# Three small lone stages of a two-block transformer kernel are taken into their neighbours

## The reference, cut to what matters

```
h = x
proj = rmsnorm(h, norm_mix_g) @ w_in            # q, k, v, u
h = h + concat(rmsnorm(attention), rmsnorm(ssm)) @ w_out
h = h + memory_attention(rmsnorm(h), rmsnorm(mem))
h = h + peer(rmsnorm(h))
...
mod = silu(c) @ w_ada + b_ada                   # shifts sh, scales sc, gates g
h1 = rms_norm(h, norm1_g) * (1 + sc1) + sh1     # norm2 likewise with sc2, sh2
ang = positions * inv_freq;  cos, sin = cos(ang), sin(ang)
q, k = rope(rms_norm(q, qn)), rope(rms_norm(k, kn))
lam = exp(lam_q1 . lam_k1) - exp(lam_q2 . lam_k2) + 0.2
```

## Time and profile before

| | |
|---|---|
| timed executions, median | 3892.75 us |
| the profiled execution: span from its first to its last event | 3886.6 us |
| PE busy | 3642.7 us (94%) |
| DVE busy | 2969.4 us (76%) |
| ACT busy | 1709.3 us (44%) |
| POOL busy | 737.9 us (19%) |
| DMA | 853.09 MB, mean 219 GB/s |

### The profile page before, as it was taken

How to read it: one execution, slowest core, us unless ns; L and a number is a source line. 1 busy time by engine, 2 the same in 40 slices (tenths; PEclk the granted TensorE clock), 3 DMA queues, 4 the chain that set the end, 5 groups by cost and what they waited for, 6 DMA issues and landing times. The chain is left out here.

```text
span 3886.6 us, 54799 instructions
## 1 busy us (share of the span) xinstructions
PE 3642.7 (94%) x19550; PEld 3183.2 (82%) x19550; DVE 2969.4 (76%) x6481; ACT 1709.3 (44%) x3206; POOL 737.9 (19%) x523
## 2 busy tenths in 40 slices
PE   7877899999999999999798999989999999999998
PEld 6545677899999988888687766778999999888887
DVE  3654463599888889999677576444998888799998
ACT  3512343234566643333354455332335666533333
POOL 0000000000333334444100000000002333345442
PEclk9978999999999999999898999999999999999999
DMA  4261222355899999999532102222557999899997
GB/s 130 84 217 44 87 90 76 115 163 167 272 309 307 304 344 405 404 402 399 194 99 64 65 8 76 65 87 96 163 166 238 314 309 310 306 402 404 404 404 285
DMA packets 371790, 853.09 MB, mean 219 GB/s; under 512 B 36016, under 2 KB 185136, under 8 KB 368944
## 3 DMA queue, kind: packets, MB, share of 16 engines
q1 hardware_dynamic: 258816, 530.45, 39.3%
q0 software_dynamic: 73728, 268.47, 18.2%
q10 hardware_dynamic: 38976, 50.68, 3.8%
HBM read 753.91 MB, written 94.37 MB: 218 GB/s over the span
## 5 line engine op out<-in xcount | busy, mean ns | idle before, releaser
L1150 POOL DMA_INDIRECT p2f_row<-in_expert_u_rows,p2f_index x128 | 174.4, 1362 | 1351.1 <-POOLq L83 1078.2
L1150 POOL DMA_INDIRECT p1f_row<-in_peer_u_rows,p1f_index x128 | 179.5, 1402 | 1006.8 <-POOLq L83 707.8
L1766 PE MATMUL p2v_out<-p2a_u_hi,p2v_w_hi 128*128 128x512 f32 x768 | 299.2, 390 | 0.4 <-DVE p2v_w_lo L1747 0.4
L1766 PE MATMUL p1v_out<-p1a_u_hi,p1v_w_hi 128*128 128x512 f32 x768 | 299.2, 390 | 0.0
L1766 PE MATMUL p2v_out<-p2a_u_lo,p2v_w_hi 128*128 128x512 f32 x768 | 299.2, 390 | 0.0
L1766 PE MATMUL p1v_out<-p1a_u_hi,p1v_w_lo 128*128 128x512 f32 x768 | 299.2, 390 | 0.0
L1766 PE MATMUL p1v_out<-p1a_u_lo,p1v_w_hi 128*128 128x512 f32 x768 | 299.2, 390 | 0.0
L1766 PE MATMUL p2v_out<-p2a_u_hi,p2v_w_lo 128*128 128x512 f32 x768 | 299.1, 390 | 0.0
L1150 POOL DMA_INDIRECT p2f_row<-in_expert_v,p2f_index x128 | 203.5, 1590 | 238.1 <-DVE p2f_sum L1173 217.2
L1725 ACT CAST p1a_u_hi<-p1a_u 128x1024 fp32r<-128x1024 f32 x128 | 135.1, 1055 | 254.9 <-PE p1v_out L1766 246.6
L1150 POOL DMA_INDIRECT p1f_row<-in_peer_v,p1f_index x128 | 175.3, 1370 | 235.1 <-DVE p1f_sum L1173 213.8
(11 more groups left out here) (737 smaller groups left out, 10905.9 us busy)
## 6 DMA issues: line engine op xcount, KB each, us to landing
p1a_u<-in_peer_u SPq DMA_DIRECT2D x128, 512.0 KB, 4.3
p1a_u<-in_peer_v SPq DMA_DIRECT2D x128, 512.0 KB, 9.4
p2a_u<-in_expert_u SPq DMA_DIRECT2D x128, 512.0 KB, 4.1
p2a_u<-in_expert_v SPq DMA_DIRECT2D x128, 512.0 KB, 10.1
gates<-p_kept SPq DMA_DIRECT2D x20, 2048.0 KB, 12.0
acts<-p1a_a ACTq DMA_DIRECT2D x128, 192.0 KB, 4.3
p1w_a<-acts SPq DMA_DIRECT2D x128, 192.0 KB, 7.9
acts<-p2a_a ACTq DMA_DIRECT2D x128, 192.0 KB, 4.3
```

The lines of the kernel that those rows point to most:

```text
L1150: self.nc.gpsimd.indirect_dma_start(self.row[:, n % self.RING, :], None, self.u_rows if dot else self.v_rows, bass.IndirectOffsetOnAxis(ap ...
L1766: last = nc.tensor.matmul(out[:, o, :], lhs[:, s, t * P:(t + 1) * P], rhs[:, n % VSLABS, cols], start=(n == 0 and m == 0), stop=(n == KEYS ...
```

## The change

- x is loaded in four parts of 512 KB, one for each token tile, issued by SP in the first stage (now `opening`) right behind `cols`. The stage doesn't wait for them; in n0, ACT waits for part t before it squares tile t. The stage `load` is gone. The four semaphores belong to the outermost level and are cleared at the end of the program.
- The stage `rope_tables` is gone. `RopeTables`, a guest of w1, does its work in slabs 1 to 7 of the first chunk, in space of `mixT`, which is free until the attention. n0's `transfers` load its positions and `rows` (now 544 columns, 272 KB, since the gains aren't repeated). Behind w1's last slab, SP stores the tables (1 MB) to DRAM and waits, ahead of the bias; n3's `transfers` load them back in place of the 1936 KB of rows.
- The stage `scales` is gone: its two scale columns are made in `take_columns`, behind a wait for its own four additions, and `subln` beside `att_q` in the first stage.
- `mem` is loaded by n1's `transfers` instead of at the head of wmq. This isn't in the change's short title, but it is in the diff.

```diff
         self.copied = [sem("nm_copied_by_act"), sem("nm_copied_by_dve")]
         self.out = out
     def load(self, sp):
-        sp.dma_start(self.mem[:], self.mem_dram).then_inc(self.mem_in, 16)
+        pass
...
     def act(self, act, slab):
         if slab in (1, 2):
             t = slab - 1
-            act.wait_ge(self.mem_in, 16)
             if t == 1:
                 act.wait_ge(self.squared, 1)
...
             for t in range(tiles):
+                if arrived:
+                    act.wait_ge(arrived[t], 16)
                 nc.scalar.activation(xn[:, t, :], src[:, t, :], ACT.Square,
                                      accum_out=sumsq[:, t:t + 1]).then_inc(squares_done, 1)
...
-for _name, _width in (("gains", 2 * DIL_W + 2 * DIFF_W), ("inv_freq", HEAD // 2), ("lambdas", 4 * HEAD)):
+for _name, _width in (("gains", 4 * HEAD), ("inv_freq", HEAD // 2), ("lambdas", 4 * HEAD)):
...
-def constants(nc, ctx, cols_dram):
+def opening(nc, ctx, cols_dram, h, x_dram, arrived):
...
         @block.sync
         def _(sp):
             sp.dma_start(cols[:], cols_dram).then_inc(cols_in, 16)
+            for t in range(TT):
+                sp.dma_start(h[:, t, :], x_dram[:, t, :]).then_inc(arrived[t], 16)
...
             nc.vector.tensor_scalar(att_q[:], cols[:, a:a + 1], HEAD ** -0.5, None, ALU.mult)
+            nc.vector.tensor_scalar(subln[:], cols[:, b:b + 1], 1.0 - LAM_INIT, None, ALU.mult)
...
                 hT = phase_tools(nc, ctx, "b1n")[0]("hT", [P, DK, SEQ])
-                norm_transpose(nc, "n0", C, h, TT, D, hT, column(C, "norm_mix_g"))
+                rope = RopeTables(nc, A, mixT, lam_neg)
+                norm_transpose(nc, "n0", C, h, TT, D, hT, column(C, "norm_mix_g"), transfers=rope.sources(),
+                               arrived=arrived)
...
+                        ahead=rope.store, inside=[rope, heads])
...
-        memory_attention(nc, C, h, hT, A)
+        sb, _, _ = phase_tools(nc, ctx, "b1m")
+        hT, mem = sb("hT", [P, DK, SEQ]), sb("mem", [P, MEM_LEN // P, D])
+        norm_transpose(nc, "n1", C, h, TT, D, hT, column(C, "norm_mem_g"),
+                       transfers=[(mem[:], A["mem"].rearrange("(t p) d -> p t d", p=P))])
+        memory_attention(nc, C, h, hT, mem, A)
...
+                                         self.C["cols"][:, ab + 8 * src:ab + 8 * src + 8],
+                                         ALU.add).then_inc(self.columns_taken, 1)
+        dve.wait_ge(self.columns_taken, MODS)
+        for i, name in enumerate(("norm1_g", "norm2_g")):
+            a = COLS[name][0]
+            self.nc.vector.scalar_tensor_tensor(self.C["scales"][:, i, :], self.mods[:, 2 * i + 1, :], 1.0,
+                                                self.C["cols"][:, a:a + 8], ALU.add, ALU.mult)
...
+class RopeTables:
...
+    def store(self, sp):
+        sp.wait_ge(self.made, 1)
+        sp.dma_start(self.A["rope"], self.tables).then_inc(self.stored, 16)
+        sp.wait_ge(self.stored, 16)
...
+    def act(self, act, slab):
+        if slab == 3:
+            act.wait_ge(self.ready, 1)
+            self.nc.scalar.activation(self.sinb, self.red, ACT.Sin).then_inc(self.sined, 1)
+            self.nc.scalar.activation(self.s_half, self.half, ACT.Sin).then_inc(self.sined, 1)
+        if slab == 4:
+            self.nc.scalar.activation(self.edots, self.dots, ACT.Exp).then_inc(self.exped, 1)
...
+    def tables_of(self, kinds):
+        for kind in kinds:
+            gain = self.rows[:, kind * HEAD:(kind + 1) * HEAD].unsqueeze(1).broadcast_to([P, TT, HEAD])
+            for half in range(2):
+                cols = slice(self.F * half, self.F * half + self.F)
+                for table, angle in ((self.cosg, self.cosb), (self.sing, self.sinb)):
+                    last = self.nc.vector.scalar_tensor_tensor(table[:, :, kind, cols], angle, KIND_SCALES[kind],
+                                                               gain[:, :, cols], ALU.mult, ALU.mult)
+        return last
...
+    def dve(self, dve, slab):
+        V, F = self.nc.vector, self.F
+        if slab == 1:
+            self.ch = ch = Chain(dve, self.v)
+            f0, l0 = ROWS["inv_freq"][0], ROWS["lambdas"][0]
+            ch.add(V.tensor_copy(self.posf, self.posi))
+            lams = self.rows[:, l0:l0 + 4 * HEAD].rearrange("p (a b d) -> p a b d", a=2, b=2)
+            ch.add(V.tensor_tensor(self.prod, lams[:, :, 0, :], lams[:, :, 1, :], ALU.mult))
...
+            ch.add(V.tensor_reduce(self.dots, self.prod, AX.X, ALU.add))
+            ch.add(V.tensor_tensor(self.ang, self.posf.unsqueeze(2).broadcast_to([P, TT, F]),
+                                   self.rows[:, f0:f0 + F].unsqueeze(1).broadcast_to([P, TT, F]), ALU.mult))
...
+        if slab == 2:
+            sincos_reduced(V, self.ch, self.ang, self.turns, self.red)
+            V.tensor_scalar(self.half, self.red, 0.5, None, ALU.mult).then_inc(self.ready, 1)
...
+        if slab == 5:
+            ch = self.ch
+            dve.wait_ge(self.sined, 2)
+            ch.add(V.tensor_tensor(self.sq, self.s_half, self.s_half, ALU.mult))
             ch.wait()
+            ch.add(V.tensor_scalar(self.cosb, self.sq, -2.0, 1.0, ALU.mult, ALU.add))
+            dve.wait_ge(self.exped, 1)
+            ch.add(V.tensor_tensor(self.diff, self.edots[:, 1:2], self.edots[:, 0:1], ALU.subtract))
...
+            V.tensor_scalar(self.lam_neg[:], self.diff, -LAM_INIT, None, ALU.add)
+        if slab == 6:
+            self.tables_of((0, 1))
+        if slab == 7:
+            self.tables_of((2, 3)).then_inc(self.made, 1)
...
         qkT = sb("qkT", [P, QK2_TILES, SEQ])
-        lam_neg = sb("lam_neg", [P, 1])
         with ExitStack() as ctx:
-            sbr, _, _ = phase_tools(nc, ctx, "b2r")
-            cosg, sing = (sbr(n, [P, TT, len(GAIN_AT), HEAD]) for n in ("cosg", "sing"))
-            with ExitStack() as ctx2:
-                rows = phase_tools(nc, ctx2, "b2s")[0]("rows", [P, NROWS])
-                norm_transpose(nc, "n3", C, h, TT, D, hT, lambda k: scale1[:, k:k + 1], lambda k: mods[:, 0, k:k + 1],
-                               transfers=[(rows[:], A["rows"].partition_broadcast(P))])
-                rope_tables(nc, C, A, cosg, sing, rows, lam_neg)
+            rope = phase_tools(nc, ctx, "b2r")[0]("rope", [P, 2, TT, len(GAIN_AT), HEAD])
+            cosg, sing = rope[:, 0], rope[:, 1]
+            norm_transpose(nc, "n3", C, h, TT, D, hT, lambda k: scale1[:, k:k + 1], lambda k: mods[:, 0, k:k + 1],
+                           transfers=[(rope[:].rearrange("p a t k d -> p (a t k d)"), A["rope"])])
             queries_keys(nc, C, hT, A["w_qk_2"], cosg, sing, qkT)
         oaT = sb("oaT", [P, 2, SEQ])
...
 def program(nc, A, stop=None):
     with ExitStack() as ctx:
-        C = constants(nc, ctx, A["cols"])
-        sb, _, _ = phase_tools(nc, ctx, "main")
+        sb, _, sem = phase_tools(nc, ctx, "main")
         h = sb("h", [P, TT, D])
-        load(nc, "x", [(h[:], A["x"].rearrange("(t p) d -> p t d", p=P))])
+        arrived = [sem(f"arrived{t}") for t in range(TT)]
+        C = opening(nc, ctx, A["cols"], h, A["x"].rearrange("(t p) d -> p t d", p=P), arrived)
         mods = sb("mods", [P, MODS, DK])
         g1 = sb("g1", [P, D])
         g2 = sb("g2", [P, D])
         C["scales"] = sb("scales", [P, 2, DK])
-        C["subln"] = sb("subln", [P, 1])
-        block1(nc, C, h, A, Modulation(nc, C, A, mods, g1, g2))
-        scales(nc, C, mods)
-        block2(nc, C, h, mods, g1, g2, A)
+        lam_neg = sb("lam_neg", [P, 1])
+        block1(nc, C, h, A, arrived, Modulation(nc, C, A, mods, g1, g2), lam_neg)
+        block2(nc, C, h, mods, g1, g2, A, lam_neg)
```

More of the change, by code:

```diff
@@ L990, in _, with norm_transpose @@
                 finish(dve, i)
-def norm_transpose(nc, tag, C, src, tiles, width, dst, scale, bias=None, transfers=()):
+def norm_transpose(nc, tag, C, src, tiles, width, dst, scale, bias=None, transfers=(), arrived=()):
     kt = width // P
@@ L2335, in column, with block1 @@
     return lambda k: C["cols"][:, a + k % width:a + k % width + 1]
[L2338 to L2353 removed]
+def block1(nc, C, h, A, arrived, modulation, lam_neg):
     with ExitStack() as mid:
@@ new lines, with __init__, sources, place @@
+class RopeTables:
+    F = HEAD // 2
+    def __init__(self, nc, A, space, lam_neg):
+        self.nc, self.A, self.lam_neg = nc, A, lam_neg
+        flat = space[:].rearrange("p a b -> p (a b)")
+        self.tables = flat[:, 0:ROPE]
+        self.cosg, self.sing = (flat[:, n * ROPE // 2:(n + 1) * ROPE // 2].rearrange("p (t k d) -> p t k d", t=TT, d=HEAD)
+                                for n in range(2))
+        self.rows = flat[:, ROPE:ROPE + NROWS]
+        at = ROPE + 2 * BANK
+        self.posi = flat[:, at + 900:at + 900 + TT].bitcast(I32)
+        spare = lambda n: flat[:, at + TT * self.F * n:at + TT * self.F * (n + 1)].rearrange("p (t f) -> p t f", t=TT)
+        (self.ang, self.turns, self.red, self.half, self.s_half, self.sq) = (spare(n) for n in range(6))
```

(30 more changed lines are left out.)

109 lines of the change are left out of this document (20 added, 89 removed).

## The result

In the comparison that gave the result, the changed kernel took 3868.14 us (median of 6 runs, 3860.58 to 3870.84) and the kernel before 3887.47 us (median of 6, 3877.93 to 3895.26): 0.995 of the time, interval 0.9937 to 0.9963, 19.3 us less. The forecast of 3869.7 us was 1.6 us off. Two errors cancel in that: the gain was to be 23 us and was 19, and the starting point, 3892.75 us from three runs, was 5 us above what more runs of the same kernel give (3887.69 us, median of 29). So that the figure came out within 1.6 us is luck; what can be judged is the gain, 19.3 against 23.05 us. One run of the kernel before in the second group of experiments, 4204.72 us, fell into a slower state and is left out.

What follows compares the result with a forecast made beforehand. PE is busy 94% of the span, so only its idle time between stages can be won. Terms -8.0, -5.05, -0.6, -10.5, +0.5 and +0.6 sum to -23.05 us, giving a 3869.7 us median; range 3862 to 3877 us.

Steps and rivals of the forecast that it cites:

- Opening: Program start through n0: x issued earlier in four parts lets everything behind start sooner, -8.0 us (bounds -8.7 and -6.5).
- third square: n0 on ACT: third square ready at 8.95 us, where today the rehearsal starts at 16.98 us.
- rival of parts in a row: Opening: x's four parts don't overlap, last at 11.6 to 17.0 us; time 3871 to 3878 us; chance 0.09.
- Guest in w1: First chunk of w1: the rope-table work fits beside the product, DVE 17.9 and ACT 12.2 of 21.76 us; cost 0.
- tight place of the forecast: Head of w1: slab 3's `w_lo` ready at 38.4 us, PE there at 40.1 us, 1.7 us to spare.
- rival of a late w1: w1's first chunk: DVE becomes the bound; 3895 us at twice the guest's price; chances 0.03 late, 0.02 late and slower.
- wmq: Start of wmq without `mem` ahead: first split 3.1 us sooner and 1.95 us from the clock, -5.05 us.
- the clock's, -1.95 us: First matmuls of wmq: with shorter idle time PE comes back at full instead of half clock, -1.95 us.
- `scales` and `rope_tables`: Around block 2: removing both stages gains their time on the timeline, -0.6 and -10.5 us.
- Program's end: After the last stage: clearing x's four semaphores with one more barrier costs +0.5 us (0 to 0.8).
- Clock at the moved starts: Starts of wmq and qk: one chance in six each of a 1.7 us clock loss, +0.6 us (0 to 3.4).
- sign of being wrong: Second trace: another stage gets longer though nothing in it was edited; no size given.

Runs made afterwards that it cites:

- after_one_x: Changed kernel with x loaded as one 2 MB DMA in the first stage instead of four parts: 3872.0 us, 0.9966 of the kernel before.
- after_long: Changed kernel with 18 instead of 10 pairs of rehearsal matmuls at most product starts: 3869.21 us, 0.9947 of the kernel before.
- before_long: Kernel before with 18 instead of 10 pairs of rehearsal matmuls at most product starts: 3888.73 us, 1.0003 of the kernel before.
- long_double: after_long with the guest's angle reduction and 16 table products in w1 done twice: 3871.76 us (one run).
- opening_only: Kernel before with only the four early loads of x, awaited tile by tile in n0: 3884.96 us, 0.9996 of the kernel before.
- rope_scales_only: Kernel before with only the rope tables and scale columns moved; x's stage and mem's place unchanged: 3883.87 us, 0.999 of the kernel before.
- mem_only: Kernel before with only the load of mem moved from the head of wmq to n1: 3881.96 us, 0.9986 of the kernel before.
- before_again: Kernel before, unedited, run and profiled a second time: 3884.72 us (one run).
- before_bridge: Kernel before with three more rehearsal pairs after the first weight slab lands, at each product's start: 3883.7 us, 0.9992 of the kernel before.
- after_again: Changed kernel, unedited, run and profiled a second time: 3868.59 us, 0.9945 of the kernel before.

## Why the prediction was right

**Opening, forecast -8.0 us: measured -7.9 and -7.3** (w1 at 19.31 and 20.1 against 27.21 and 27.4 us). The third square was to be ready at 8.95 us, the rehearsal started at 8.79; the transposes were to start near 13.3, they did at 13.21. The assumption that carried it, that four parts move as the one does, holds: 7.7 against 7.9 us here, 8.5 at most in the other traces. The rival of parts in a row (the last at 11.6 us or later) is out. The Trainium skill ("DMA: Bandwidth & Descriptors", Bandwidth), which wants 1 MiB and more for each DMA, would have kept the one load; after_one_x is that version, its w1 starts 3 to 4 us later, and its median is 3.4 us higher.

**Guest in w1, forecast 0: measured 0.** In after_long, where the clock is full, w1 takes 99.4 us against 99.3 in before_long, and PE never waits in chunk 0. These are its eight slabs, in the columns of the earlier trace rows, and the tight place of the forecast:

```profile
25.13:46.89 21.76, 21.73 (x96) 18.03 (x97) 16.82 (x48) 11.82 (x21) 0.00 (x0) 1.00 0.53 174
...
27.70 1.28 ACT L2666 ACT_TABLE_LOAD   x1
30.27 0.31 ACT L2666 ACTIVATE b_mixT<-b_mixT 128x128 f32<-128x128 f32 x1 [1.29 <-DVE b_mixT L2697]
...
30.76 0.68 DVE L284 TENSOR_TENSOR w_w_lo<-w_w,w_w_hi 128x512 fp32r<-128x512 f32 x1
```

DVE is busy for 16.8 us (forecast 17.9), ACT for 11.8 (12.2). The sine does wait for DVE, and slab 3's `w_lo` ends at 31.44 us; PE needs it at 25.16 + 3 x 2.72 = 33.3 us, 1.9 us to spare where the forecast had 1.7. In after, the root's table comes back at 89.13 us and still leaves ACT 0.53 us of waiting for PE before its next split, and the bias is issued at 87.78 us, 5.7 us behind the store of the tables: both as estimated, and hidden. The rival of a late w1 put the point at which it decides at 1.5 times the guest's work, and 25 us of loss at twice: at 12 us of guest in place of 7, long_double shows one wait and w1 0.7 us longer, with PEclk 1.00 before and behind it. That rival's price was far too high, since one short wait at the end of the guest's work isn't one in every slab.

**wmq, forecast -5.05 us: measured -3.4.** The term that was mis-sized is the clock's, -1.95 us. (Its own figures, nine intervals and a first one, add up to -2.06; with full clock restored, wmq is 1.3 to 1.8 us shorter still, 51.8 to 52.0 against 53.3 to 53.6 us.) I reasoned that idle time of 2.27 us leaves the clock full because w1 showed it once. One row in one trace can't say that: w1 itself was hit in five of eight unbridged traces.

**`scales` and `rope_tables`, forecast -11.1 us: measured -10.6** (544.9 us on average in the seven traces without the two stages, 555.5 us in the seven with them). qk starts 0.7 us behind n3's last copy. In `take_columns` the two products end at 260.9 us and `take_row` behind them idles 2.06 us for PE: covered.

**Program's end, forecast +0.5 us: measured +0.4 to 0.5** (from the first store of `out` to the end of the span 17.7 to 17.8 us against 17.3).

**Clock at the moved starts, forecast +0.6 us: too small, and wrong in kind.** I looked only at wmq and qk. Nearly half of all such starts are hit, in both kernels, each for 1.6 to 2 us (w1 101.0 against 99.4, pa 18.9 against 17.3, gl 103.7 against 102.1, vb 52.3 against 50.3). In the traces shown, after has six hits and the first of before had one. This is the sign of being wrong that I had named, a stage longer though nothing in it was edited: va and vb are. And the change isn't neutral in it, since it takes the half-clock rehearsal from qk. The four unbridged traces with the stage `rope_tables` have 15 hits together, the four without it 19: one more each, or some 1.7 us (my estimate, from these counts and the price of a hit; four traces on either side can't show so small a difference).

These terms sum to -7.9 - 3.4 - 10.6 + 0.5 = -21.4 us; the two traces of after are 17.5 and 19.8 us shorter than the first of before, and the medians 19. The 2 to 4 us between are within what the clock and the ssm tables (102.1 to 110.4 us, over both kernels alike; `take_columns`, some 0.4 us on DVE, is the only edit there) do to a run.

**What stays open.** The single edits' medians don't add up. opening_only gives 1.3 us, rope_scales_only 3.8, mem_only 4.3: 9.4 us together, where the whole gives 19. Their intervals are some 3.5 us to either side each, so the three together are known to about 6 us (my estimate, errors taken as independent), the whole to 5: the two differ by more than chance in the medians makes likely, though not by much more. Each trace shows its gain in full at the edited place, and loses it in stages that weren't edited: half-clock starts, a longer p2. With the starts bridged the opening's median gain is still only 2.4 us, though its profiled execution is 7.6 us shorter, so hits behind rehearsals alone don't explain it. Whether such losses meet the single edits by chance or follow from where they leave the later stages, 11 runs and one trace of each can't tell. So the sum of the parts rests on the traces, the total on the medians of after, and the share of each edit in that total is not settled.

## What to carry to other kernels

A small stage between two barriers costs its whole length on the critical engine, waits for its DMA included. Here the same work was free inside a product that had the engines free for as long, and the sum from the timeline (busy time of the guest plus that of the host, and the first slab at which both meet) says so to within 0.2 us. Issue a load where its queue is idle, one stage before it is needed, and in as many parts as its reader has tiles (shown here for parts of 512 KB). And don't read the clock behind a short wait from one trace: take two, and count the starts; where a stage in front is taken out, look whether the rehearsal behind it now ends early.

## What the runs showed of the hardware that was not expected

- Behind 2.5 us of rehearsal and about 2 us of idle time, the granted clock fell to half (PEclk 0.57 to 0.67 over the next 4 us) in 34 of 75 starts, at other starts in each run of the same kernel. None of these 34 had idled less than 1.85 us. With a long rehearsal or a bridge it fell in 2 of 54, after 1.23 and 2.20 us of idle time; the other 52 had 1.07 us or less at a time. gl was hit in all eight unbridged traces, p1q and p2q in none. The Trainium skill ("TensorE: Matmul & The Clock Gate", What's actually happening) says that the number of slow matmuls at a kernel's start varies from run to run; the traces show the like at the stages' starts, and add that the stage's own pattern weighs as well.
- A rehearsal that itself ran at half clock (0.50 to 0.62) filled the wait as a bridge does: the first real matmul came 4.1 to 5.2 us behind its start, like the 4.2 to 5.6 us behind most warm ones, and PEclk was 0.81 to 1.00 in all 28 such starts with 1.1 us of idle time or less. Of five with 1.3 to 1.7 us, two were at 0.50 and 0.61.
- Four DMAs of 512 KB that load x in after, issued within 1.84 us, landed 1.26 to 1.28 us apart, the first 3.8 us behind its issue. A store of that size takes 2.6 us, so my forecast's rival took its price from the other direction; a single load of 512 KB with nothing beside it is in no trace.
- The stage of the ssm tables takes 102 to 110 us in one and the same kernel. Its granted clock tells most of the traces apart. These are the 10 us that begin 80 us into it in before_again (102.8 us) and in after_one_x (108.4 us):

```profile
255.50:265.50 10.00, 8.53 (x76) 4.84 (x73) 5.34 (x16) 1.72 (x3) 0.00 (x0) 1.00 0.25 30
...
251.60:261.60 10.00, 10.00 (x51) 5.93 (x53) 1.02 (x3) 1.72 (x3) 0.00 (x0) 0.50 0.01 2
```

  PEclk is 1.00 there in all nine traces of 102.1 to 105.4 us, 0.50 to 0.57 in the three longest and in before_bridge (106.1 us); but after_again has 1.00 with 106.8 us, so it isn't the clock of this stretch alone. The only edit in this stage is that of `take_columns`, and long and short traces are found with it and without.
